# Eight more half units ahead of the second half of the first layer's input projection, and streamed columns in couples of 512

## The reference

```python
mod = (silu(c) @ w_ada[l] + b_ada[l])              # 6 vectors of 2048, from the condition c
h = rms_norm(x) * (1.0 + sc1) + sh1
z = h @ w_in[l]                                    # one input projection for three head groups
da_q, da_k, da_v, q_a, kv_a, k_rope, sg_u, sg_v = split(z)
out_a = diff_attention(da_q, da_k, da_v, ...)      # 6 heads, two softmaxes each, ALiBi bias
out_b = latent_attention(q_a, kv_a, k_rope, ...)   # q_a (512 wide) -> queries, kv_a (256) -> keys, values
out_c = spatial_gating(sg_u, sg_v, ...)            # 4 groups of 128
x = x + g1 * (concat(out_a, out_b, out_c) @ w_out[l])
h = rms_norm(x) * (1.0 + sc2) + sh2
x = x + g2 * conv_ffn(h, ...)                      # 2048 -> 2 x 5632 -> 2048
```

## Time and profile before

| | |
|---|---|
| median of 3 runs | 2428.52 us (2427.35 to 2429.77) |
| the profiled execution | 2429.96 us |
| its span | 2427.8 us |
| PE busy | 2334.6 us, 96% |
| PE weight load busy | 2046.1 us, 84% |
| DVE busy | 1845.4 us, 76% |
| ACT busy | 1143.5 us, 47% |
| POOL busy | 299.7 us, 12% |
| mean granted TensorE clock | 0.986 |

### The profile page before, as it was taken

How to read it: one execution, slowest core, us unless ns; L and a number is a source line. 1 busy time by engine, 2 the same in 40 slices (tenths; PEclk the granted TensorE clock), 3 DMA queues, 4 the chain that set the end, 5 groups by cost and what they waited for, 6 DMA issues and landing times.

```text
span 2427.8 us, 38206 instructions
## 1 busy us (share of the span) xinstructions
PE 2334.6 (96%) x15360; PEld 2046.1 (84%) x15360; DVE 1845.4 (76%) x2555; ACT 1143.5 (47%) x1613; POOL 299.7 (12%) x437
## 2 busy tenths in 40 slices
PE   5889999999999999999999999998999999999999
PEld 2578988888888888888888889988888888888888
DVE  1656877879998889889887685767998667766775
ACT  1333654455543455345544356545454345544553
POOL 3221321211101000100031121011110000000000
PEclk8899999999999999999999999999999999999999
DMA  9988787968889888988886877555896556655654
GB/s 334 331 295 278 251 286 239 318 200 281 292 288 328 267 261 261 297 297 253 266 260 218 276 235 232 167 191 178 276 291 223 191 190 190 190 189 188 190 191 148
DMA packets 450656, 597.03 MB, mean 246 GB/s; under 512 B 24188, under 2 KB 398128, under 8 KB 450224
## 3 DMA queue, kind: packets, MB, share of 16 engines
q1 hardware_dynamic: 394784, 392.54, 50.0%
q0 software_dynamic: 55296, 201.35, 25.2%
q10 hardware_dynamic: 400, 0.71, 0.1%
HBM read 592.42 MB, written 2.10 MB: 245 GB/s over the span
## 4 chain that ended last, share of the span: by engine, by line
PE 72%; DVE 14%; DMA 5%; issue 5%; ACT 3%; POOL 1%; DVEq 0%; ACTq 0%; POOLq 0%
PE bank L1134 72%; DVE wlo L1706 4%; DVE acc L1700 3%; DMA ada<-in_w_ada_dram 3%; DMA raw<-in_w_in_dram 2%; ACT whi L1459 2%; DVE T L1725 1%; DVE yg L1732 0%; DVE T L1789 0%; DVE r L1774 0%; ACT hx L1527 0%; DVE yv L1732 0%; ACT sc_s L1580 0%; DVE yv L1733 0%; DVE mx L1742 0%
## 5 line engine op out<-in xcount | busy, mean ns | idle before, releaser
L1134 PE MATMUL bank<-hx,whi 128*128 128x512 f32 (+1 forms) x4480 | 1361.4, 364 | 5.5 <-ACT z L1459 2.8
L1706 DVE TENSOR_TENSOR wlo<-raw,whi 128x1024 fp32r<-128x1024 f32 (+2 forms) x774 | 908.3, 1179 | 435.5 <-ACT whi L1459 434.1
L1459 ACT ACTIVATE whi<-raw 128x1024 fp32r<-128x1024 f32 (+2 forms) x774 | 779.6, 1017 | 788.9 <-PE bank L1134 738.7
L1134 PE MATMUL bank<-hx,wlo 128*128 128x256 f32 x3840 | 1088.5, 284 | 31.9 <-DVE hx L1810 21.3
L1134 PEld LDWEIGHTS bank<-hx,whi 128*128 128x128 f32 x4480 | 803.7, 190 | 145.0 <-issue 8.0
L1134 PEld LDWEIGHTS bank<-hx,wlo 128*128 128x128 f32 x3840 | 732.0, 191 | 50.2 <-issue 21.3
L1134 PE MATMUL bank<-mx,whi 128*128 128x512 f32 (+1 forms) x2096 | 612.3, 356 | 1.4 <-DVE xT L1756 1.4
L1134 PE MATMUL bank<-mx,wlo 128*128 128x256 f32 x1728 | 486.3, 281 | 0.0
L1134 PEld LDWEIGHTS bank<-mx,whi 128*128 128x128 f32 x2096 | 370.4, 189 | 61.7 <-issue 4.8
L1095 POOL DMA_DIRECT2D ada<-in_w_ada_dram x367 | 223.7, 611 | 1433.5 <-DVE acc L1700 911.9
L1134 PEld LDWEIGHTS bank<-mx,wlo 128*128 128x128 f32 x1728 | 327.6, 190 | 1.9 <-issue 1.2
(11 more groups left out here) (171 smaller groups left out, 1297.4 us busy)
## 6 DMA issues: line engine op xcount, KB each, us to landing
ada<-in_w_ada_dram POOLq DMA_DIRECT2D x367, 512.0 KB, 5.5
raw<-in_ffn_w_up_dram SPq DMA_DIRECT2D x352, 512.0 KB, 4.6
raw<-in_ffn_w_down_dram SPq DMA_DIRECT2D x176, 512.0 KB, 4.3
raw<-in_w_in_dram SPq DMA_DIRECT2D x128, 512.0 KB, 5.0
raw<-in_w_out_dram SPq DMA_DIRECT2D x48, 512.0 KB, 4.4
first_ada<-in_w_ada_dram POOLq DMA_DIRECT2D x17, 512.0 KB, 17.6
raw<-in_w_out_dram SPq DMA_DIRECT2D x32, 256.0 KB, 4.0
raw<-in_mla_w_uq_dram SPq DMA_DIRECT2D x12, 384.0 KB, 4.5
```

Source lines behind the costliest of these rows:

```text
L1134: return pe.matmul(out_, lhsT, rhs, start=start, stop=stop, skip_group_check=True)
L1459: return act.activation(out_, in_, ACT.Copy)
L1706: i_ = tt(dst, src, high.bitcast(F32), ALU.subtract)
```

## The change

- **QA moves.** In the first layer, pairs 9 and 10 join the early pairs: their k 0 to 7 are four more units (20 to 23) before phase 1 begins, their k 8 to 15 are units 44 to 47, added by `addz`. The late pairs of the first layer are then SGV, SGU and kr. The items that make h of k 8 to 15 are queued four units before the end of phase 0, as before they were queued two before it. There are 66 units up to the end of the first projection, as before.
- **Couples.** Pairs 6 and 7 of DAV, and pairs 14 and 15 of SGV, become one wide pair each (WIDE_PAIRS), in both layers: units of two k by 512 columns, a step of three matmuls of 512 columns into one whole bank, one copy or `addz` of 512 instead of two of 256. Pair 8 stays as it was.
- **Heads.** In the first layer the heads of differential attention follow each other every two and a half units and not every three, and `dak` 0 and 1 stand in one group.
- **Spreading of mod's work** after batch 2 starts at the wide SGV pair (unit 48) and not at pair 10 (unit 44), in the first layer.

```diff
 TOKEN_PAIRS = DAV_PAIRS + SGV_PAIRS
 
 TWO_PAIRS = DAQ_PAIRS + DAK_PAIRS
-EARLY_PAIRS = DAQ_PAIRS + DAK_PAIRS + DAV_PAIRS + (KVA_PAIR,)
-SPREAD_FROM = (QA_PAIRS[1], QA_PAIRS[1])
-LATE_PAIRS = QA_PAIRS + SGV_PAIRS + SGU_PAIRS + ("kr",)
+WIDE_PAIRS = (DAV_PAIRS[0], SGV_PAIRS[0])
+FRONT_PAIRS = DAQ_PAIRS + DAK_PAIRS + (DAV_PAIRS[0], DAV_PAIRS[2], KVA_PAIR)
+EARLY_PAIRS = (FRONT_PAIRS + QA_PAIRS, FRONT_PAIRS)
+LATE_PAIRS = (SGV_PAIRS[:1] + SGU_PAIRS + ("kr",), QA_PAIRS + SGV_PAIRS[:1] + SGU_PAIRS + ("kr",))
+SPREAD_FROM = (SGV_PAIRS[0], QA_PAIRS[1])
+
+
+def home(pair):
+
+    return pair - 1 if pair - 1 in WIDE_PAIRS else pair
+
+
+def k_steps(pair, k0, k1):
+    step = 2 if pair in WIDE_PAIRS else 4
+    return [(pair, k, step) for k in range(k0, k1, step)]
...
-    return 1 if l == 0 and pair in EARLY_PAIRS else 0
+    return 1 if l == 0 and home(pair) in EARLY_PAIRS[0] else 0
...
-                at.setdefault(x * space + s_, []).append((-s_, toks))
+                at.setdefault(int(x * space) + s_, []).append((-s_, toks))
...
-        order = [(a, 0), (b, 0), (a, 4), (b, 4)] + [(pair, k0) for pair in EARLY_PAIRS[2:] for k0 in (0, 4)]
...
+        order = [(a, 0, 4), (b, 0, 4), (a, 4, 4), (b, 4, 4)] + [x for pair in EARLY_PAIRS[0][2:] for x in k_steps(pair, 0, 8)]
...
             if n == 2:
-                self.ada_over(2, len(order) - 4)
+                self.ada_over(2, 16)
...
-            if n == len(order) - 2:
+            if n == len(order) - 4:
                 self.ada_flush()
                 groups = self.item_groups(0, "n1", range(8, 16), 2)
                 self.queue.extend([[("onep", 0, 0, 8, 16)] + groups[0]] + groups[1:])
...
-        ks = (8, 12) if l == 0 else (0, 4, 8, 12)
-        a, b = EARLY_PAIRS[:2]
-        order = [(a, 8), (b, 8), (a, 12), (b, 12)] if l == 0 else []
-        order += [(pair, k0) for pair in EARLY_PAIRS[2:] for k0 in ks]
...
+        k_first = 8 if l == 0 else 0
+        a, b = EARLY_PAIRS[l][:2]
+        order = [(a, 8, 4), (b, 8, 4), (a, 12, 4), (b, 12, 4)] if l == 0 else []
+        order += [x for pair in EARLY_PAIRS[l][2:] for x in k_steps(pair, k_first, KC)]
+        for pair, k0, kt in order:
+            self.unit("win", l, pair, 0, k0, kt, k0 == k_first, k0 + kt == KC, win_phase(l, pair))
+            if k0 + kt < KC:
                 continue
...
-                self.queue.extend([("dak", l, v), ("dakmul", l, v)] for v in range(3))
-                self.queue.extend(self.heads(l, 0, NH, 3))
+                if l == 0:
+                    self.queue.extend([[("dak", l, 0), ("dakmul", l, 0), ("dak", l, 1), ("dakmul", l, 1)],
+                                       [("dak", l, 2), ("dakmul", l, 2)]])
+                else:
+                    self.queue.extend([("dak", l, v), ("dakmul", l, v)] for v in range(3))
+                self.queue.extend(self.heads(l, 0, NH, 2.5 if l == 0 else 3))
...
-        for pair in LATE_PAIRS:
+            if pair == QA_PAIRS[-1]:
+                self.second.extend(self.stats(l, J_QA))
+        for pair in LATE_PAIRS[l]:
             if pair == SPREAD_FROM[l]:
 
-                self.ada_over(5 if l == 0 else 11, 4 * len(LATE_PAIRS[LATE_PAIRS.index(pair):]) - 3 + 20 + 4)
+                units = sum(1 if x == "kr" else len(k_steps(x, 0, KC)) for x in LATE_PAIRS[l][LATE_PAIRS[l].index(pair):])
+                self.ada_over(5 if l == 0 else 11, units + 20 + 4)
...
-            for k0 in (0, 4, 8, 12):
-                self.unit("win", l, pair, 0, k0, 4, k0 == 0, k0 == 12, 0)
+            for _, k0, kt in k_steps(pair, 0, KC):
+                self.unit("win", l, pair, 0, k0, kt, k0 == 0, k0 + kt == KC, 0)
...
-            if pair == SGV_PAIRS[-1]:
+            if pair == SGV_PAIRS[0]:
...
+            if pair not in WIDE_PAIRS:
+                return ch(z, 2 * pair + c_)
+            return ch(z, 2 * pair, 4).rearrange("p (a c n) -> p a c n", a=2, c=2)[:, :, c_, :]
+
+        def pair_bank(pair, b):
+            return b[:, 0:512].rearrange("p (a n) -> p a n", a=2) if pair in WIDE_PAIRS else b[:, 0:S]
...
+                    width = 512 if x_.i in WIDE_PAIRS else 256
...
+                            elif x_.what == "win" and x_.i in WIDE_PAIRS:
+                                a, ca = o + j * 512, 2 * k * S + c_ * P
+                                mm(b[:, 0:512], hx[:, ca:ca + P], whi[:, a:a + 512], start, False)
+                                mm(b[:, 0:512], hx[:, ca:ca + P], wlo[:, a:a + 512], False, False)
+                                i_ = mm(b[:, 0:512], hx[:, ca + S:ca + S + P], whi[:, a:a + 512], False, stop)
...
-                    copy(ch(z, 2 * pair + c_), b[:, 0:S]).then_inc(emptied_act, 1)
+                    copy(z_of(pair, c_), pair_bank(pair, b)).then_inc(emptied_act, 1)
...
                     l, w = t[1:]
-                    for pair in (SGU_PAIRS, SGV_PAIRS)[w]:
+                    for pair in (SGU_PAIRS, SGV_PAIRS[:1])[w]:
                         wait_emptied(act, ("win", l, pair, 1, 0))
                     act.activation(ch(z, 24 + 4 * w, 4), ch(z, 24 + 4 * w, 4), ACT.Gelu_apprx_tanh).then_inc(sg_act, 1)
```

More of the change, by code:

```diff
@@ L289, in unit @@
             self.pop()
-            self.ada(Unit(*f).kt / (16 if f[0] == "kr" else 4))
+            self.ada(Unit(*f).kt / (16 if f[0] == "kr" else 2 if f[0] == "win" and f[2] in WIDE_PAIRS else 4))
         u = len(self.units)
@@ L365, in build @@
             self.add("first", min(n + 1, SPLITS))
-        a, b = EARLY_PAIRS[:2]
-        order = [(a, 0), (b, 0), (a, 4), (b, 4)] + [(pair, k0) for pair in EARLY_PAIRS[2:] for k0 in (0, 4)]
-        for n, (pair, k0) in enumerate(order):
+        a, b = EARLY_PAIRS[0][:2]
+        order = [(a, 0, 4), (b, 0, 4), (a, 4, 4), (b, 4, 4)] + [x for pair in EARLY_PAIRS[0][2:] for x in k_steps(pair, 0, 8)]
+        for n, (pair, k0, kt) in enumerate(order):
             if n == 2:
-                self.ada_over(2, len(order) - 4)
+                self.ada_over(2, 16)
             if n == 6:
@@ L381, in build @@
                 self.queue.extend([[("onep", 0, 0, 8, 16)] + groups[0]] + groups[1:])
-            self.unit("win", 0, pair, 0, k0, 4, k0 == 0, k0 == 4, 0)
-            if k0 == 4:
+            self.unit("win", 0, pair, 0, k0, kt, k0 == 0, k0 + kt == 8, 0)
+            if k0 + kt == 8:
                 for c in range(2):
@@ L396, in projection @@
         if l > 0:
-            self.transition(l, "n1", [("win", l, pair, 0) for pair in EARLY_PAIRS[:2]])
-            for pair in EARLY_PAIRS[:2]:
+            self.transition(l, "n1", [("win", l, pair, 0) for pair in EARLY_PAIRS[l][:2]])
+            for pair in EARLY_PAIRS[l][:2]:
                 for c in range(2):
                     self.add("copy", l, pair, c, 0)
-        ks = (8, 12) if l == 0 else (0, 4, 8, 12)
-        a, b = EARLY_PAIRS[:2]
-        order = [(a, 8), (b, 8), (a, 12), (b, 12)] if l == 0 else []
-        order += [(pair, k0) for pair in EARLY_PAIRS[2:] for k0 in ks]
-        for pair, k0 in order:
-            self.unit("win", l, pair, 0, k0, 4, k0 == ks[0], k0 == 12, win_phase(l, pair))
-            if k0 < 12:
+        k_first = 8 if l == 0 else 0
[5 more added lines that the diff above has]
+            if k0 + kt < KC:
                 continue
@@ L976, in words @@
             x = units[u]
+            if x.what == "win" and x.i in WIDE_PAIRS:
+                return x.kt * 512
             return {"kr": 512, "ukv": 1024, "uq": 768}.get(x.what, x.kt * 256)
@@ L1434, in _ @@
                     if i < NH and h % 2 == 0:
-                        pair = DAV_PAIRS[h // 2]
+                        pair = home(DAV_PAIRS[h // 2])
                         wait_emptied(pe, ("win", l, pair, 1, win_phase(l, pair)))
@@ L1711, in _ @@
                     b = wait_full(dve, ("win", *t[1:]))
-                    a = ch(z, 2 * pair + c_)
+                    a = z_of(pair, c_)
                     if pair in TWO_PAIRS:
                         order.after(tt(a, b[:, S:2 * S], a, ALU.add))
-                    tt(a, b[:, 0:S], a, ALU.add).then_inc(emptied_dve, 1)
+                    tt(a, pair_bank(pair, b), a, ALU.add).then_inc(emptied_dve, 1)
                 elif kind == "copy" and t[2] in TWO_PAIRS:
```

1 line of the change is left out of this document (added).

## The result

The changed kernel is slower. Its median is 2438.65 us (10 runs, 2433.33 to 2444.14), beside 2430.03 for the kernel before on the same chip (10 runs, 2427.35 to 2434.44). The ratio is 1.0029, with a 95% interval of 1.0020 to 1.0038, so about 7 us lost where 7.8 were forecast as gain. The profiled execution is the longest of the ten (2444.14), 14.5 longer in its span than the profiled one before, so sections of the trace are compared here, and not only its sum.

What follows compares the result with a forecast made beforehand. PE was taken as the bound, busy 96% of the span. Terms -8.0 - 3.4 + 1.6 + 1.5 + 0.5 = -7.8 gave 2420.7 us from the median of 2428.52; eight-in-ten range 2415.5 to 2428.

Steps and rivals of the forecast that it cites:

- part 4: Layer 0 heads every 2.5 units: +1.5 us (0 to 5), DVE 93% for 87%; mod's later spread +0.5 (0 to 2).
- The transition to the FFN is not touched: End of the output projection: no cost there, as the last of batch 4 is still summed before the transition.
- part 1: Wait at units 20 to 23, from 160 us: QA's first halves fill it, all gained, -8.0 us (4.5 to 8.5).
- the 49 matmuls of 170:180: Stage 170 to 180 us: PE busy at clock 0.86 with 49 matmuls, where the stages before had 86 and 98.
- 2, wide steps: 112 steps of 512 columns outside phase 0 save 30 ns each, -3.4 us (0 to 5.0).
- 3, two `dak` in one bank: Second `dak` waits 0.9 us for the first's bank, longer idle may stretch low clock: +1.6 us (0.9 to 3.0).
- Lie beside units in a stretch where PE does not wait: QA's four `addz` on DVE, replacing copies on ACT, 0.42 us each: placed where PE does not wait.
- D: Dense heads make DVE late beyond its 6 us: heads and mod's work 5 + 2, `dak` 3.0; 2427, chance 0.12.
- F: Heads 2 to 5: bias on POOL bounds, DVE waits some 15 us, 10 reach PE; 2434, chance 0.08.
- the first wait of PE after 110 us at `dak`: Expected sign in the profile: with the stage 160:180 filled, PE's first wait after 110 us comes at `dak`.

## Why the prediction was wrong, point by point

The forecast was 2420.7; slower by more than 0.2% had a chance of 0.09. Two steps failed. The larger is in part 4, "The work for mod is spread from unit 48 on and no longer from 44, so four `acc` of 1.28 and a burst come later ... 0 to 2 us, I take 0.5", with the sentence behind it, "The transition to the FFN is not touched". It counted the work that moves and not what it moves beside. Moved alone it costs 7 us (1.0029), in the changed kernel 10.7 and without the couples 6, for the 0.5 of the sum; with QA early and heads every three units it was only 3. The rest of the change was put at -8.3 and measured -3.6 (0.9985, the kernel with mod's work from unit 44, interval -1.2 to -6.1); that gap is the second step, in part 1, "so all of what is filled is gained". The last burst of batch 4 came four units nearer to the transition, among the `padd` of POOL, behind which its loads queue; and `acopy` 2 came behind `exp` 5 and `gelu` on ACT. Both places were to be read from the order of the instructions. Nor can the plan catch up: it places one part of mod's work beside a unit at most, so a late start is a late end.

**1, the hole, -8.0.** Right for the place: eight units in 22.84 us, unit 28 at the time worked out, no wait for `hx`. One reading was wrong without harm: the 49 matmuls of 170:180 were held against the 86 and 98 of the stages before, but half of these are 512 columns wide, and by the row of units 23 and 24 full clock gives 58 of them in 10 us. Wrong was "so all of what is filled is gained". With couples left out and mod's work put back, the change is at 1.0007: with what it brings at the `dak` and in the heads, nothing of the 8.5 remains. Where they went shows in the kernel with mod's work from unit 44, beside the kernel before with four units of QA (11.5 us) counted where they now stand. From unit 20 to the first unit of DAV's second half it took 53.3 us for 58.4, so 5.1 of the 8.5 arrive there, and 3.4 are lost again in a stretch whose wait is that for the late weights at units 32 and 33 (DMA share 1.03 to 1.05); from there to unit 48 it took 57.7 for 54.4, and from 48 to 66 78.9 for 77.6. What is left is half a microsecond, with an estimated 1.3 of the couples in it. The late weights were to be seen in the earlier trace rows, where the share is 1.06 until the hole begins: a unit of 512 KB in 2.85 us with one load of mod of 512 KB beside it wants 368 GB/s by estimate, and the full stages moved 356 to 371. The hole had been the pause in which loads ran ahead.

**2, wide steps, -3.4.** Right: 28 ns a step for the 30 forecast, and the two couples alone are worth 2.9 us in one timing (0.9988) and 4.6 in the other (0.9981). The rule of the Trainium skill (TensorE: Matmul & The Clock Gate, section Back-to-back issue gap) for the isolated gap, by which a joined pair saves one fixed part of 2.5 ns and the whole an estimated 0.8 us, is not borne out by this trace: 12 matmuls less in a unit saved 0.11 us, some 9 ns each. The measurement decides.

**3, two `dak` in one bank, +1.6.** The waits are as forecast (1.98 and 0.94), the low clock is not: from 238.80 to 249.00 it was 0.50 (0.67 in the kernel with mod's work from unit 44), where 1.7 us had been allowed for one slow unit. By units 36 to 48 of five traces the term was 3 to 5 (57.7 with the pair for 53.7 and 52.6 apart, 54.4 for 51.6).

**4, heads, +1.5.** In the right range (1.0011 alone, 2 to 3 us), and DVE was 93% busy as worked out (58.33 of 63.0 us, 249 to 312), but by other waits than `wlo`: ACT's `sq` behind `exp` with its table load (1.02 at 260.80), and `addz` of QA on DVE behind its chain (1.41 at unit 48 in the kernel with mod's work from 44). "Lie beside units in a stretch where PE does not wait" was wrong for these four.

Of the rivals, D (dense heads take back the gain) was near for part 3 and too high for the heads; it put 2 us on mod's work, the others no more than the sum did. F (the bias as bound), the only one that was slower, did not occur: DVE shows no wait for a bias in the heads. The chance of 0.09 for slower so rested almost wholly on something that didn't happen, and "the first wait of PE after 110 us at `dak`" was wrong too, since PE waited 1.4 for `sq` at 207.15.

## What to carry to other kernels

When a schedule made of slots is shifted, look at what each moved instruction now stands behind on every in-order engine, the one that issues DMAs above all; that costs more than its own time. Work taken from one place to fill a hole had been cover where it stood: count what it covered, and what the engines and DMA queues did while the hole lasted. Parts of a change that serve each other (QA early, the pair of `dak`, dense heads) must be priced together, and parts that don't (the couples) are best tried alone: here these were the gain.
